# A router with its weights as the stationary side, two low parts on GpSimd, and more of the second up loaded early

## What is computed

```python
def hierarchical_moe(x, w_rg, b_rg, w_re, b_re, w_gate, w_up, w_down):
    glog = (xf @ w_rg + b_rg).astype(jnp.float32)
    gsel = jnp.argmax(glog, axis=-1)
    ...
    elog_all = (xf @ w_re + b_re).astype(jnp.float32).reshape(n, N_GROUPS, EXPERTS_PER_GROUP)
    topv, topi = lax.top_k(elog, TOP_K)
    tw = jax.nn.softmax(topv, axis=-1) * pg
    ...
    for e in range(N_EXPERTS):
        h = jax.nn.silu(xf @ w_gate[e]) * (xf @ w_up[e])
        y = y + combine[:, e:e + 1] * (h @ w_down[e])
```

## Time and profile before

| | us |
|---|---|
| median of 3 runs (913.95 to 917.6) | 917.16 |
| the profiled execution | 917.69 |
| its span, first to last instruction | 916.0 |
| TensorE busy | 856.5 |
| VectorE busy | 426.7 |
| ScalarE busy | 213.6 |
| GpSimd busy | 3.7 |

### The profile page before, as it was taken

How to read it: one execution, slowest core, us unless ns; L and a number is a source line. 1 busy time by engine, 2 the same in 40 slices (tenths; PEclk the granted TensorE clock), 3 DMA queues, 4 the chain that set the end, 5 groups by cost and what they waited for, 6 DMA issues and landing times.

```text
span 916.0 us, 11255 instructions
## 1 busy us (share of the span) xinstructions
PE 856.5 (94%) x4601; PEld 554.7 (61%) x4601; DVE 426.7 (47%) x804; ACT 213.6 (23%) x387; POOL 3.7 (0%) x17
## 2 busy tenths in 40 slices
PE   5999999999999999999999965999996799999986
PEld 4888888877777888888734522354642353644532
DVE  6428416577665344436888222314433214435123
ACT  5422222364444222213211100001100001100114
POOL 0000000000000100000000000000000000000000
PEclk9999999999999999999999977999998899999999
DMA  9343322121213653593489999999999999999995
GB/s 331 83 92 92 103 82 92 47 93 47 92 47 92 206 118 107 208 393 125 184 310 425 407 431 426 426 423 421 430 423 424 429 428 428 426 429 427 426 413 196
DMA packets 67958, 246.85 MB, mean 269 GB/s; under 512 B 22168, under 2 KB 45760, under 8 KB 54336
## 3 DMA queue, kind: packets, MB, share of 16 engines
q1 hardware_dynamic: 67824, 246.07, 68.8%
q10 hardware_dynamic: 80, 0.02, 0.0%
HBM read 243.98 MB, written 2.10 MB: 269 GB/s over the span
## 4 chain that ended last, share of the span: by engine, by line
PE 84%; DMA 9%; DVE 3%; issue 1%; ACT 1%; SPq 0%; DVEq 0%; ACTq 0%
PE bank L837 18%; PE bank L549 10%; PE bank L551 10%; PE bank L550 10%; PE bank L889 8%; DMA R<-w_down 5%; PE bank L821 4%; DMA R<-w_gate 3%; PE bank L578 3%; PE bank L576 3%; PE bank L577 3%; PE bank L917 2%; PE bank L918 1%; PE bank L636 1%; DVE h_tok L1776 1%
## 5 line engine op out<-in xcount | busy, mean ns | idle before, releaser
L837 PE MATMUL bank<-R,packT 128*64 128x512 f32 (+1 forms) x1004 | 186.5, 607 | 17.3 <-issue 7.9
L837 PEld LDWEIGHTS bank<-R,packT 128*64 128x64 f32 (+1 forms) x1004 | 57.7, 129 | 127.9 <-issue 127.3
L1300 DVE TENSOR_TENSOR wlo<-raw,whi 128x2048 fp32r<-128x2048 f32 x33 | 75.5, 2287 | 85.5 <-ACT whi L1051 85.4
L549 PE MATMUL bank<-xnT_hi,whi 128*128 128x512 f32 x288 | 113.7, 395 | 0.7 <-DVE wlo L1300 0.7
L551 PE MATMUL bank<-xnT_hi,wlo 128*128 128x512 f32 x288 | 112.2, 390 | 0.0
L550 PE MATMUL bank<-xnT_lo,whi 128*128 128x512 f32 x288 | 112.1, 389 | 0.0
L889 PE MATMUL bank<-R,actT 128*64 128x512 f32 (+1 forms) x416 | 82.0, 637 | 15.5 <-DMA R<-w_down 15.2
L1051 ACT ACTIVATE whi<-raw 128x2048 fp32r<-128x2048 f32 x34 | 64.9, 1909 | 67.4 <-PE bank L551 38.7
L889 PEld LDWEIGHTS bank<-R,actT 128*64 128x64 f32 (+1 forms) x416 | 24.9, 135 | 66.9 <-issue 66.3
L1767 DVE SCALAR_TENSOR_TENSOR y_lo<-bank,small,y_hi 128x512 fp32r<-128x512 f32 x26 | 19.4, 750 | 93.1 <-ACT y_hi L1204 93.1
L549 PEld LDWEIGHTS bank<-xnT_hi,whi 128*128 128x128 f32 x288 | 54.1, 188 | 12.1 <-issue 1.5
(11 more groups left out here) (298 smaller groups left out, 1217.0 us busy)
## 6 DMA issues: line engine op xcount, KB each, us to landing
R<-w_up SPq DMA_DIRECT2D x30, 2048.0 KB, 16.6
R<-w_gate SPq DMA_DIRECT2D x26, 2048.0 KB, 20.2
R<-w_down SPq DMA_DIRECT2D x23, 2048.0 KB, 19.4
raw<-w_in SPq DMA_DIRECT2D x18, 1024.0 KB, 5.1
R<-w_down SPq DMA_DIRECT2D x12, 1024.0 KB, 9.1
R<-w_gate SPq DMA_DIRECT2D x8, 1024.0 KB, 10.6
raw<-w_in SPq DMA_DIRECT2D x16, 256.0 KB, 4.3
raw<-w_branch_a SPq DMA_DIRECT2D x4, 1024.0 KB, 5.2
```

The lines of the kernel that those rows point to most:

```text
L549: pe.matmul(dst, hi_w, hi_x, start=start, stop=False)
L837: mm = pe.matmul(dst[s * w:(s + 1) * w, :], packT[:, c, odd * P + s * w:odd * P + (s + 1) * w], part_of(s, c) if part_of else R[2 * slots[ ...
L1300: dve.tensor_tensor(wlo[c % 2][:, :], raw[c % 2][:, :], whi[c % 2][:, :].bitcast(F32), ALU.subtract).then_inc(lo_split, 1)
```

## The change

Five edits, which share the same 25 us of the program.

1. **Router.** `route(t)` now has `w_router[:, c, :]` (36 columns) as the stationary side and streams the 128 columns of `hgT`. Even blocks go to partitions 0 to 35 of PSUM and odd ones to 64 to 99, so that two sums of four blocks arise, with the tokens along the columns. ScalarE copies the two into `logitsT` (two instructions a tile), and `turn_logits` multiplies by `fold` (two shifted pieces of the identity, added), which adds the halves and turns them. `logitsT` is cleared once and `fold` made once, by VectorE.
2. **Low parts.** `low_h(0)` and `low_h(1)` leave VectorE. GpSimd scales `hg` by `rstd` in place and subtracts `hn_hi`, one tile after the other.
3. **Gather.** All four high parts come first, then low 0, low 1, low 2 and 3.
4. **Loads.** Four gate blocks of the first pair go to `gate_block` 0 to 3, so that 5 of 8 blocks of `R[0]` and 5 of 8 of `R[1]` take the second pair's up early (before: 4 and 2). What is left, 3 and 3 blocks, waits for the half of the first gate alone.
5. **A wait.** `gate_block` 0 and 1 lie under `weight_a`; VectorE writes the first weights only after the first four matmuls of the gate (`gate_first_done`).

```diff
@@ -114,6 +114,7 @@
     first_gate = at("first_gate", [P, 8 * DE], F32, 8)
+    gate_block = [at(f"gate_block{j}", [P, DE], F32, kb) for j, kb in enumerate((214, 216, 206, 196))]
     gate_rest = at("gate_rest", [P, 2 * DE], F32, 200)
@@ -127,6 +128,8 @@
     squares = at("squares", [P, 512], F32, 216)
+    logitsT = at("logitsT", [P, TT, P], F32, 209.5)
+    fold = at("fold", [P, NR], F32, 219.53125)
     logits = at("logits", [P, TT, NR], F32, 198)
@@ -337,7 +343,7 @@
-        PARTED = {0: 48, 4: 48, 5: 64, 6: 64, 7: 64, 10: 64}
+        PARTED = {0: 112, 4: 32, 5: 64, 6: 64, 7: 64, 10: 64}
@@ -406,23 +412,30 @@
             wait_unit_used(sp, WO - 2)
-            sp.dma_start(first_gate[:, :], flat(w_gate, 0)).then_inc(slot_loaded[0], 16)
+            sp.dma_start(first_gate[:, DE:8 * DE], flat(w_gate, 0)[:, DE:8 * DE]).then_inc(slot_loaded[0], 16)
             sp.dma_start(first_down[0][:, :], flat(w_down, 0)[:, 0:4 * DE]).then_inc(slot_loaded[2], 16)
-            sp.dma_start(R[0][:, 0:4 * DE], flat(w_up, 2)[:, 0:4 * DE]).then_inc(spare_loaded, 16)
+            sp.dma_start(R[0][:, 0:5 * DE], flat(w_up, 2)[:, 0:5 * DE]).then_inc(spare_loaded, 16)
             load_unit(UNITS - 2)
             wait_unit_used(sp, WO - 1)
             sp.wait_ge(merged_ready, KT)
             load_step(1, w_up, 0, 1)
             load_unit(UNITS - 1)
-            sp.dma_start(R[1][:, 0:6 * DE], flat(w_gate, 1)[:, 0:6 * DE]).then_inc(slot_loaded[0], 16)
+            sp.dma_start(R[1][:, DE:4 * DE], flat(w_gate, 1)[:, DE:4 * DE]).then_inc(slot_loaded[0], 16)
+            sp.dma_start(gate_block[0][:, :], flat(w_gate, 0)[:, 0:DE]).then_inc(slot_loaded[0], 16)
+            sp.dma_start(gate_block[2][:, :], flat(w_gate, 1)[:, 4 * DE:5 * DE]).then_inc(slot_loaded[0], 16)
             sp.dma_start(gate_rest[:, :], flat(w_gate, 1)[:, 6 * DE:8 * DE]).then_inc(slot_loaded[0], 16)
-            sp.dma_start(R[1][:, 6 * DE:8 * DE], flat(w_up, 3)[:, 6 * DE:8 * DE]).then_inc(spare_loaded, 16)
+            sp.dma_start(R[1][:, 4 * DE:8 * DE], flat(w_up, 3)[:, 4 * DE:8 * DE]).then_inc(spare_loaded, 16)
+            sp.dma_start(R[1][:, 0:DE], flat(w_up, 3)[:, 0:DE]).then_inc(spare_loaded, 16)
             sp.dma_start(R[5][:, :], flat(w_down, 1)).then_inc(slot_loaded[2], 16)
             sp.wait_ge(dve_tile_done, 24)
             sp.dma_start(R[7][:, :], flat(w_gate, 3)).then_inc(slot_loaded[3], 16)
+            sp.wait_ge(hsq_summed, 2 * TT)
+            sp.dma_start(gate_block[1][:, :], flat(w_gate, 1)[:, 0:DE]).then_inc(slot_loaded[0], 16)
             sp.wait_ge(logits_done, TT)
+            sp.dma_start(gate_block[3][:, :], flat(w_gate, 1)[:, 5 * DE:6 * DE]).then_inc(slot_loaded[0], 16)
             sp.dma_start(R[6][:, :], flat(w_gate, 2)).then_inc(slot_loaded[3], 16)
-            sp.wait_ge(hn_lo_ready, TT)
+            sp.wait_ge(hn_lo_early, 2)
+            sp.wait_ge(hn_lo_ready, TT - 2)
             sp.dma_start(first_down[1][:, :], flat(w_down, 0)[:, 4 * DE:8 * DE]).then_inc(spare_loaded, 16)
@@ -463,9 +476,11 @@
                             sp.wait_ge(HALF_DONE[m4], i4 + 1)
+                            if k == 4:
+                                sp.dma_start(R[0][:, 5 * DE:8 * DE], flat(w, e[0])[:, 5 * DE:8 * DE]).then_inc(slot_loaded[0], 16)
+                                sp.dma_start(R[1][:, DE:4 * DE], flat(w, e[1])[:, DE:4 * DE]).then_inc(slot_loaded[0], 16)
+                                continue
                             if k == 6:
-                                load_half(k, 0, w, e[0], 1)
-                            elif k == 4:
                                 load_half(k, 0, w, e[0], 1)
@@ -473,10 +488,7 @@
                                 load_half(k, 0, w, e[0], 1)
-                            if k == 4:
-                                sp.dma_start(R[1][:, 4 * DE:6 * DE], flat(w, e[1])[:, 4 * DE:6 * DE]).then_inc(slot_loaded[0], 16)
-                            else:
-                                load_half(k, 1, w, e[1], 1)
+                            load_half(k, 1, w, e[1], 1)
                             continue
@@ -529,6 +541,13 @@
                                pattern=[[1, P]], channel_multiplier=-1).then_inc(route_iotas_made, 1)
+            pool.wait_ge(rstd_ready, 1)
+            for t in range(2):
+                pool.wait_ge(hn_hi_ready, t + 1)
+                pool.tensor_scalar(hg[:, t, :, :], hg[:, t, :, :], rstd[:, t:t + 1], None, ALU.mult).then_inc(hg_scaled, 1)
+                pool.wait_ge(hg_scaled, t + 1)
+                pool.tensor_tensor(hn_lo[:, t, :, :], hg[:, t, :, :], hn_hi[:, t, :, :].bitcast(F32), ALU.subtract
+                                   ).then_inc(hn_lo_early, 1)
@@ -742,9 +761,14 @@
                 for c in range(KT):
-                    mm = pe.matmul(bank[t][:, 0:NR], hgT[t // 2][:, c, (t % 2) * P:(t % 2 + 1) * P],
-                                   w_router[:, c, :], start=(c == 0), stop=(c == KT - 1))
-                mm.then_inc(logits_done, 1)
+                    mm = pe.matmul(bank[t][c % 2 * 64:c % 2 * 64 + NR, P:2 * P], w_router[:, c, :],
+                                   hgT[t // 2][:, c, (t % 2) * P:(t % 2 + 1) * P], start=(c < 2), stop=(c >= KT - 2))
+                mm.then_inc(logitsT_done, 1)
+
+            def turn_logits(t):
+
+                pe.wait_ge(logitsT_copied, 2 * t + 2)
+                pe.matmul(bank[t][:, 0:NR], logitsT[:, t, :], fold[:, :], start=True, stop=True).then_inc(logits_done, 1)
@@ -753,13 +777,17 @@
-            pe.wait_ge(router_scaled, 1)
+            pe.wait_ge(router_scaled, 2)
             route(0)
+            route(1)
             turn_h(2)
-            route(1)
             turn_h(3)
             route(2)
+            turn_logits(0)
+            turn_logits(1)
             route(3)
+            turn_logits(2)
+            turn_logits(3)
@@ -798,16 +826,15 @@
                 def add_low(t):
-                    pe.wait_ge(hn_lo_ready, t + 1)
+                    pe.wait_ge(hn_lo_early, t + 1)
                     for c in range(KT):
                         add_part(hn_lo, t, c)
-                add_high(0)
+                for t in range(TT):
+                    add_high(t)
                 add_low(0)
-                for t in range(1, TT):
-                    add_high(t)
                 add_low(1)
-                pe.wait_ge(hn_lo_ready, TT)
+                pe.wait_ge(hn_lo_ready, TT - 2)
                 for c in range(KT):
@@ -837,14 +864,20 @@
                                        start=(c == 0), stop=(c == KT - 1))
+                    if first_done is not None and c == 0:
+                        mm.then_inc(first_done, 1)
                     if half_done is not None and c == KT // 2 - 1:
                         mm.then_inc(half_done, 1)
                 mm.then_inc(done, 1)
             def first_gate_part(s, c):
-                tile = first_gate if s == 0 else R[1] if c < 6 else gate_rest
-                c = c - 6 if tile is gate_rest else c
-                return tile[:, c * DE:(c + 1) * DE]
+                if c == 0:
+                    return gate_block[s][:, :]
+                if s == 1 and c in (4, 5):
+                    return gate_block[c - 2][:, :]
+                if s == 1 and c >= 6:
+                    return gate_rest[:, (c - 6) * DE:(c - 5) * DE]
+                return (R[1] if s else first_gate)[:, c * DE:(c + 1) * DE]
@@ -868,7 +901,7 @@
                 if half_done is not None:
-                    pe.wait_ge(spare_loaded, 48)
+                    pe.wait_ge(spare_loaded, 64)
                     for c in range(FT):
@@ -968,7 +1001,8 @@
                 project(main, slots_of(i, 0), odd, bank[0], main.gate_done, packed=None if odd else i + 1,
-                        half_done=gate_half_done if i < 3 else None, part_of=None if i else first_gate_part)
+                        half_done=gate_half_done if i < 3 else None, part_of=None if i else first_gate_part,
+                        first_done=None if i else gate_first_done)
                 if i == 0:
@@ -1173,9 +1207,20 @@
             square_h(1, 3)
+            def copy_logitsT(t):
+                act.wait_ge(logitsT_done, t + 1)
+                for half in range(2):
+                    part = slice(half * 64, half * 64 + NR)
+                    act.activation(logitsT[part, t, :], bank[t][part, P:2 * P], ACT.Copy).then_inc(logitsT_copied, 1)
+
+            act.wait_ge(logitsT_cleared, 1)
+            copy_logitsT(0)
             copy_hgT(2, 0)
+            copy_logitsT(1)
             copy_hgT(3, 0)
             copy_hgT(3, 1)
+            copy_logitsT(2)
+            copy_logitsT(3)
             scale_h(2)
@@ -1512,6 +1557,8 @@
                               ALU.mult).then_inc(router_scaled, 1)
+            dve.memset(logitsT[:, :, :], 0.0).then_inc(logitsT_cleared, 1)
+            dve.tensor_tensor(fold[:, :], ident[:, 0:NR], ident[:, 64:64 + NR], ALU.add).then_inc(router_scaled, 1)
             for t in range(TT):
```

(4 more changed lines are left out.)

5 lines of the change are left out of this document (4 added, 1 removed).

## The result

The changed kernel takes **920.05 us** (median of 20 runs, 917.14 to 922.46); the kernel before, run beside it, 915.83 us (20 runs, 913.58 to 919.24). The ratio is **1.0047**, 95% interval 1.0037 to 1.0057: slower, by less than half a per cent, with an interval clear of 1. The predicted time was 919.8 us. That the two times are 0.25 us apart is luck: the prediction added 2.6 us to a median of 917.16 (3 runs), and the difference measured is 4.2 us over 915.83 (20 runs). A base 1.3 us too high made up for most of a sum 1.6 us too low. The profiled execution took 921.38 us (span 919.6), 3.7 over the 917.69 of before.

A forecast was written before the change was run, and what follows sets the result against it. The saturated expert-weight stream, started by TensorE's first gate, was taken as the bound; +2.0 (turns on VectorE) and +0.6 (gather) made +2.6 us over the 917.16 median, so 919.8 us, with an 8-in-10 range of 914.0 to 922.8.

The forecast's parts named there:

- What bounds the kernel: Expert weights are one saturated stream started by TensorE; the kernel's end moves by the same microseconds as the first gate.
- The router, TensorE side: Turned router matmuls take 0.93 us a tile instead of 1.71; last logit 1.8 us earlier, hidden by VectorE's wait.
- GpSimd and VectorE: At norm_h(1), GpSimd's SBUF reads and VectorE's two-input work take turns; the choice of experts starts 2.0 us later.
- The sign that the prediction named: In the profile after, gaps in VectorE between the norm_h(1) instructions that match GpSimd's instructions.
- The order of the gather: With all high parts first, TensorE waits 0.6 us for the second row matrix; gather 8.5 instead of 7.94 us.
- The clock: Rival: 4.6 us idle after the warming matmuls lowers TensorE's clock in the gather; up to 2 us more, 921.8; chance 0.08.
- the likeliest case: Turns on VectorE as summed, plus the gather's order: 919.8 us, own range 917.3 to 921.0, chance 0.47.
- Loads, memset, `fold`, `gate_first_done`: The extra megabyte loaded early, the two added VectorE steps and the added wait were each taken as worth nothing.
- no blocking: Rival: VectorE is not held by GpSimd, or always goes first; -1.2 us, 916.0; chance 0.19.
- quick GpSimd: Rival: GpSimd takes 1.0 us an instruction; +0.1 us, 917.3; chance 0.18, shared with weaker blocking.
- slow GpSimd: Rival: GpSimd instructions take 10.8 us each, the gate comes 20 us late, 937 us; chance 0.02.
- the pairs don't overlap: Rival: router matmul pairs don't overlap, last logit at 445.9; 919.8 us with blocking, 919.2 without; no chance given.

The follow-up runs named there:

- the last pair: Changed kernel without GpSimd work, one low part ahead of the logits, old gather order; router turned (ratio 0.9994 to the kernel before) or as before (1.0009).
- x3: Changed kernel with nine warming matmuls on TensorE in place of five; ratio to the kernel before 1.0047.
- x7: Changed kernel with the gather's old order, GpSimd work and turned router kept; ratio to the kernel before 1.0023.
- x4: Changed kernel with the old router (hgT stationary, 36 columns streamed, no fold), GpSimd work kept; ratio to the kernel before 1.0021.

## Why the prediction was right, point by point

**What bounds the kernel**: right. The end moved by 3.7 us and the first gate by 3.76, and the stream is as full as before. That the two agree to a tenth is partly luck, since the stretch behind the gate differed by 1 us and more among the runs.

**The router, TensorE side**: the price per tile was right (0.93 put down; 0.94 measured for the first two, 1.07 and 1.03 for the others). The last logit came 1.24 us earlier and not 1.8. The terms that were too small: `route(3)` started at 441.18, not 440.7, and the copy and the last two `fold` matmuls put its end at 443.26, not 442.6. Neither mattered, since VectorE was 3 us later. That the gain is hidden was forecast, and the old router in the changed kernel shows it (A 11.20 in both). That it exists where VectorE is on time, the last pair shows.

**GpSimd and VectorE**: the mechanism was right and the total good (+2.0 put down, +2.15 measured), but the number is luck: it comes from two errors against each other. The step that failed is the term for the scaling. It was put at 1.2 us, from the 0.29 us of a 128x128 affine select, and measured 2.85. It was taken to hold VectorE for all its time; in fact `gain_h(1, 3)` ran at its old 436.54 with its old 1.06 us, 1.03 us into the first scaling, and the second scaling held VectorE only until 1.1 us after its start. In the run with scalings alone nothing was held. (The first 0.9 us of a scaling stay open for two-input instructions: none began there.) The subtraction was put at 2.0 and took 2.36; it holds VectorE for its whole time, as forecast from the earlier trace rows, which had shown the other direction only. The estimate from the Trainium skill (GPSIMD Engine Reference, "Performance versus the Vector engine"), half of that page's 4497 ns for 2048 elements, was 2.2 and so a little nearer to the 2.36 measured here. The order of the turns was wrong in detail. Put down were one small instruction between the first subtraction and the second scaling, two between that and the second subtraction, and nine behind it; measured, the first was held to the end of the first subtraction, ten more came before the second, and the last was held by that. The sign that the prediction named, gaps in VectorE, did not show; long instructions stood in their place. The first gate was put at 462.4 and came at 463.59, the w_down loads at 473.7 and 474.82.

By the Trainium skill (SBUF — State Buffer, "Who interferes with whom") a VectorE instruction with two SBUF inputs contends with a GpSimd instruction that reads SBUF. The subtraction agrees, at 128x2 elements as well. The scaling, which reads `hg`, doesn't: eight two-input instructions ran inside its last 1.7 us in the changed kernel at 0.16 us each. The measurement decides.

**The order of the gather**: +0.6 put down, 0.72 to 0.76 measured.

**The clock**: this is where the sum was short. I had it as a rival, with a chance of 0.08 and up to 2 us, and not in the sum. It came true and cost 0.85 (x3 and x7, by the traces). Its condition, a long idle time, followed from the likeliest case itself: my own turns led to 4.6 us of idle time (measured: 4.35), so it was no case beside that one but a term of it, with a price from 0 to 2 us. The step that failed is to have left it out of the sum. The parts measured are 2.15 (turns), 0.76 (order) and 0.85 (clock), together the 3.76 us of the first gate.

**Loads, memset, `fold`, `gate_first_done`**: all nothing, as put down. The run with the loads alone shows it, and VectorE still waits 4.43 us for the projection behind `memset` and `fold`.

**The rivals**: "no blocking" and "quick GpSimd" are out by the three long instructions; "slow GpSimd" (10.8 us each) by 2.35 to 2.85; "the pairs don't overlap" by 0.94 us a tile. What is **still open**: how often the race at `norm_h(1)`'s last instruction falls one way and how often the other. Of the four profiles with all of GpSimd's work three show it lost (after, x7, x4) and one won (x3), and the timed runs can't be told apart by it. The old router's run (1.0021) lies 2.4 us below the changed kernel's although its profiled A + B is 0.44 less only; that run's median lies 1.7 us below its own profiled time, and its stretch behind the first gate, 455.1 us, is the shortest of all. The old order's run is alike: 2.2 us below by the ratios, 0.77 by A + B. Why is open.

## What to carry to other kernels

Work handed to an idle engine is free only if it doesn't hold what the busy one uses. Before moving an elementwise step of two SBUF inputs to GpSimd, list VectorE's instructions beside it by where their inputs are, and count each small one that meets it as held until the large one ends, as the subtraction held them here: 2.4 us of work taken away came back as 4.4 us of holding. Where two engines meet at one point, as logits do, shortening one side is worth nothing until the other is as short; and a term that makes a third engine wait longer carries the price of its clock with it, in the same sum.

## What the runs showed of the hardware

- GpSimd, 128x1024 fp32: scaling by a per-partition value 2.85 us, subtraction of two tiles 2.36, memset 0.95. The scaling, with one tensor input, is slower than the subtraction with two. VectorE does scaling and subtraction together in one instruction of 1.28.
- A held VectorE instruction is shown as busy: 2.35 us for 2 elements a partition. It is told by its length, not by an idle time.
- GpSimd's subtraction held two-input instructions (1.50, 2.35, 1.32 us). A GpSimd memset held one-input `TENSOR_SCALAR` instructions of 2 elements (0.96, 0.97), and no two-input ones. A scaling held a `TENSOR_SCALAR` until about 1.1 us after its own start (1.06, 0.88) and nothing later; one that began 0.07 us into a scaling was not held in one run (x3) and was in two others (x4, x7). Two-input instructions that began 0.98 and 1.03 us into a scaling ran unheld; for earlier ones no run shows it. Instructions that read a bank of PSUM, and reductions, were held by none.
- TensorE's granted clock after an idle time: (window 452 to 460) 1.00 after 0.96 to 1.02, 1.51 and 2.22 us; 0.79 after 3.11, 0.79 and 0.65 after 4.34 and 4.35; and 0.68 where 0.96, 0.49 and 2.68 us of idle time came close behind one another, with little work between. In the gather of the changed kernel, x7 and x4 that cost 0.4 to 0.9 us (by B, less the order's 0.72).
